# Stick-breaking attention: the value matmuls of two heads alternate on the two column halves of the array

## What is computed

```python
def block(args):                       # a block of 128 queries
    qi, bi = args
    qpos = bi * Q_BLOCK + jnp.arange(Q_BLOCK)
    mask = kpos[None, :] < qpos[:, None]
    z = jnp.einsum('bhqd,bhkd->bhqk', qi, k).astype(jnp.float32) * scale
    log_nb = jnp.where(mask, jax.nn.log_sigmoid(-z), 0.0)
    after = lax.cumsum(log_nb, axis=3, reverse=True) - log_nb
    w = jnp.where(mask, jnp.exp(jax.nn.log_sigmoid(z) + after), 0.0)
    return jnp.einsum('bhqk,bhkd->bhqd', w.astype(v.dtype), v)
```

## Time and profile before

| | |
|---|---|
| median of 3 runs | 3063.53 us (3063.17 to 3065.2) |
| span of the profiled execution | 3056.8 us |
| TensorE matmul busy | 2955.9 us, 97% |
| TensorE weight loads busy | 2375.5 us, 78% |
| VectorE busy | 1472.0 us, 48% |
| ScalarE busy | 1001.0 us, 33% |

### The profile page before, as it was taken

The page is one execution under the profiler, slowest core; times in us unless marked ns, Lnnn a source line. Parts: engine busy times, 40 slices in busy tenths (PEclk is TensorE's granted clock), DMA queues, the critical chain, the costliest instruction groups (busy, mean ns, idle before and its releaser), DMA issues. The chain is left out here.

```text
span 3056.8 us, 34380 instructions
## 1 busy us (share of the span) xinstructions
PE 2955.9 (97%) x13458; PEld 2375.5 (78%) x13458; DVE 1472.0 (48%) x1905; ACT 1001.0 (33%) x1128; POOL 32.7 (1%) x66
## 2 busy tenths in 40 slices
PE   7999999999999999999998999998999999899998
PEld 6888887478888888888776888887867567778886
DVE  6664346356743476433434444435444853443333
ACT  4222226332222322223444322224433343232222
POOL 0000000000000000000000000000000000000000
PEclk9999999899999999999999999999999999999999
DMA  4332222024333343222110222222321012222222
GB/s 161 137 131 97 106 103 82 0 96 139 136 104 110 110 144 132 93 105 85 56 42 28 96 96 96 96 102 106 131 92 64 28 55 97 83 83 96 96 102 77
DMA packets 44376, 289.99 MB, mean 95 GB/s; under 512 B 5136, under 2 KB 5520, under 8 KB 12928
## 3 DMA queue, kind: packets, MB, share of 16 engines
q1 hardware_dynamic: 35712, 259.01, 23.4%
q0 software_dynamic: 8000, 29.50, 2.9%
q10 hardware_dynamic: 576, 0.23, 0.0%
HBM read 286.62 MB, written 2.10 MB: 94 GB/s over the span
## 5 line engine op out<-in xcount | busy, mean ns | idle before, releaser
L802 DVE TENSOR_TENSOR sb_WL<-sb_RAW,sb_WH 128x2048 fp32r<-128x2048 f32 x243 | 556.8, 2291 | 891.3 <-ACT sb_WH L324 891.3
L1469 PE MATMUL PS<-sb_HH,sb_WH 128*128 128x512 f32 x2360 | 937.7, 397 | 33.8 <-DVE sb_WL L802 23.3
L1471 PE MATMUL PS<-sb_HH,sb_WL 128*128 128x512 f32 x2360 | 923.6, 391 | 0.0
L1470 PE MATMUL PS<-sb_HL,sb_WH 128*128 128x512 f32 x2360 | 923.4, 391 | 0.0
L324 ACT ACTIVATE sb_WH<-sb_RAW 128x2048 fp32r<-128x2048 f32 x243 | 464.8, 1913 | 785.1 <-PE PS L1471 783.2
L1469 PEld LDWEIGHTS PS<-sb_HH,sb_WH 128*128 128x128 f32 x2360 | 446.5, 189 | 139.6 <-issue 41.8
L1470 PEld LDWEIGHTS PS<-sb_HL,sb_WH 128*128 128x128 f32 x2360 | 446.4, 189 | 96.2 <-issue 5.0
L1471 PEld LDWEIGHTS PS<-sb_HH,sb_WL 128*128 128x128 f32 x2360 | 445.9, 189 | 94.6
L1469 PE MATMUL PS<-ff_GH,sb_WH 128*128 128x512 f32 x880 | 342.3, 389 | 0.0
L1470 PE MATMUL PS<-ff_GL,sb_WH 128*128 128x512 f32 x880 | 342.3, 389 | 0.0
L1471 PE MATMUL PS<-ff_GH,sb_WL 128*128 128x512 f32 x880 | 342.3, 389 | 0.0
(11 more groups left out here) (340 smaller groups left out, 2758.2 us busy)
## 6 DMA issues: line engine op xcount, KB each, us to landing
sb_RAW<-in_weights SPq DMA_DIRECT2D x243, 1024.0 KB, 4.8
ff_ADAW<-in_w_ada POOLq DMA_DIRECT2D x48, 512.0 KB, 4.0
sb_XT<-in_x SPq DMA_DIRECT2D x1, 2048.0 KB, 8.6
out_t<-sb_XT SPq DMA_DIRECT2D x4, 512.0 KB, 2.7
b_CT<-in_ctx POOLq DMA_DIRECT2D x1, 1024.0 KB, 5.0
hy_BD<-in_c_gates POOLq DMA_DIRECT2D x1, 512.0 KB, 3.4
hy_PT<-in_c_sel_fox POOLq DMA_DIRECT2D x1, 512.0 KB, 4.4
b_ROPE<-in_c_rope POOLq DMA_DIRECT2D x1, 512.0 KB, 6.3
```

What stands on the lines that cost most here:

```text
L802: dve.tensor_tensor(WL[slot][:, :], RAW[slot][:, :], f32(WH[slot][:, :]), ALU.subtract).then_inc(*T["w_lo"].up())
L1469: pe.matmul(out, wh, xh, start=start, stop=False)
L1470: pe.matmul(out, wh, xl, start=False, stop=False)
L1471: return pe.matmul(out, wl, xh, start=False, stop=stop)
```

## The change

The value matmuls are issued for two heads at once. `sb_values(q)` takes the heads 2q and 2q+1: for each key tile j it issues first the even head's matmul, then the odd head's, and one semaphore increment at the end. It is called in even passes h from 2 on, for q = h/2 - 1, and after the loop for the last pair. It stands where values(h-1) stood in those passes; in odd passes no value matmuls are left. `W` has three buffers in place of two, and the waits on `sb_o` count pairs: the Exp of head h waits for the pair of head h-3.

```diff
--- before.py
+++ after.py
@@ -134,7 +134,7 @@
                            ("I", [P, 4, S], F32), ("PT", [P, 2, TB, S], F32), ("BD", [P, 8, P], F32), ("B64", [P, P], F32),
                            ("MASK", [P, P], F32R), ("SEL", [P, 8, P], F32R), ("EYE", [P, P], F32R), ("ST", [P, 2, 2 * TB], F32)])
         sbm = layout("sbm", [("Q", [P, 8, S], F32), ("K", [P, 8, S], F32), ("V", [P, TB, D], F32), ("E", [P, 2, 1280], F32),
-                             ("SH", [P, 2, 1280], F32R), ("SL", [P, 2, 1280], F32R), ("W", [P, 2, 1280], F32), ("TRI", [P, P], F32R),
+                             ("SH", [P, 2, 1280], F32R), ("SL", [P, 2, 1280], F32R), ("W", [P, 3, 1280], F32), ("TRI", [P, P], F32R),
                              ("NONE", [P, P], F32R), ("MASK", [P, P], F32R), ("EYE", [P, P], F32R)])
         hyy = layout("hyy", [("YL0", [P, 4, S + 4], F32R), ("YH0", [P, 4, S], F32R), ("YH1", [P, 4, S], F32R), ("YL1", [P, 4, S], F32R)])
         HY_YH = [hyy["YH0"][:, m, :] for m in range(4)] + [hyy["YH1"][:, m, :] for m in range(4)]
@@ -591,13 +591,13 @@
                 act.wait_ge(T["sb_tri"].sem, h + 1)
                 if h == 0:
                     act.wait_ge(*T["sb_const"].now())
-                if h >= 2:
-                    act.wait_ge(T["sb_o"].sem, h - 1)
-                act.activation(sbm["W"][:, h % 2, :], zs(h)[:, 0:1280], ACT.Exp).then_inc(*T["sb_exp"].up())
+                if h >= 3:
+                    act.wait_ge(T["sb_o"].sem, (h - 3) // 2 + 1)
+                act.activation(sbm["W"][:, h % 3, :], zs(h)[:, 0:1280], ACT.Exp).then_inc(*T["sb_exp"].up())
 
             def sb_out(h):
                 if h % 2:
-                    act.wait_ge(T["sb_o"].sem, h + 1)
+                    act.wait_ge(T["sb_o"].sem, h // 2 + 1)
                     act.activation(sby["YH"][:, h // 2, :], PS[:, 6, :], ACT.Copy).then_inc(*T["y_hi"].up())
 
             split(U_SB + 1)
@@ -1719,13 +1719,19 @@
                                              start=False, stop=True, skip_group_check=True)
                 last.then_inc(*T["sb_tri"].up())
 
-            def sb_values(h):
-                pe.wait_ge(T["sb_exp"].sem, h + 1)
-                if h % 4 == 0:
-                    pe.wait_ge(T["evac"].sem, EV["sb"] + 3 * (h // 4) + 3)
-                if h >= 2 and h % 2 == 0:
-                    pe.wait_ge(T["y_ready"].sem, 8 + h // 2)
-                values(6, h, sbm["V"], lambda j: sbm["W"][:, h % 2, OFF[j]:OFF[j] + S - P * j], None).then_inc(*T["sb_o"].up())
+            def sb_values(q):
+
+                pe.wait_ge(T["sb_exp"].sem, 2 * q + 2)
+                if q % 2 == 0:
+                    pe.wait_ge(T["evac"].sem, EV["sb"] + 3 * (q // 2) + 3)
+                if q:
+                    pe.wait_ge(T["y_ready"].sem, 8 + q)
+                for j in range(TB):
+                    for e in range(2):
+                        h = 2 * q + e
+                        last = pe.matmul(PS[64 * e:64 * e + 64, 6, P * j:S], sbm["V"][:, j, HD * h:HD * h + HD],
+                                         sbm["W"][:, h % 3, OFF[j]:OFF[j] + S - P * j], start=j == 0, stop=True, skip_group_check=True)
+                last.then_inc(*T["sb_o"].up())
 
             sb_scores(0)
             for h in range(SBH):
@@ -1737,9 +1743,9 @@
                 sb_logs(h)
                 for k, s in halves[1:]:
                     half(k, s)
-                if h >= 1:
-                    sb_values(h - 1)
-            sb_values(SBH - 1)
+                if h >= 2 and h % 2 == 0:
+                    sb_values(h // 2 - 1)
+            sb_values(SBH // 2 - 1)
             pe.wait_ge(T["y_ready"].sem, 16)
             residual(RES["sb"], U_SBO, (8,), sby["YH"], sby["YL"], True)
             ffn(3)
```

## The result

The changed kernel is slower: median 3071.63 us (3066.85 to 3078.02, 6 runs) against 3063.35 us, a ratio of 1.0032 with a 95% interval of 1.0019 to 1.0045. A second set of 6 runs gave 1.0032 again (1.0014 to 1.0051). I had forecast 3057.2 us, range 3053.5 to 3064.0, with a chance of 0.11 for slower.

The account below looks back on a forecast made before the run. TensorE, busy 97% of the span, was taken to bound the kernel. Passes 1 to 11 gave -4.85 us and the last four heads -1.46, so 3063.5 - 6.3 = 3057.2 us, range 3053.5 to 3064.

Parts of the forecast that it names:

- One values block, two heads in one block: Values matmuls: one head's block takes 2.29 us; two heads on separate array halves stream together in 2.40 us.
- rivals B and D: Pair's values block: B, program order, 2.72 us, chance 0.13; D, no overlap, 4.44 us, chance 0.09.
- What it uncovers: Odd passes: scores wait 1.4 us for the Exp, starting 4.19 after logs, so each saves only 0.90 us.
- The clock: TensorE's clock at the new pauses: the sum counted no fall from them, so no cost.
- rival C: Six new 1.4 us pauses and one in pass 13 bring the clock down, 3.4 us per fall; chance 0.09.
- my -4.85: Passes 1 to 11: odd passes save 5.40 us, even passes 2 to 10 add 0.55.
- The last four heads: Passes 12 on and after the loop: +0.11, -2.72, +0.11, -0.06 and +1.1 for half clock on scores(15), together -1.46 us.
- Sum: Whole kernel: -4.85 - 1.46 = -6.3 us, taken from the median 3063.5, giving 3057.2 us.

Follow-up runs that it names:

- With the clock held: Changed kernel with 6 unread matmuls in each pause after logs(h), h odd up to 13: median 3060.11 us, ratio 0.9976 to the kernel before.
- the first profile: Beside +5.58, the changed kernel's first profile (median of its runs 3071.63 us); as the base worked from, the kernel before's, span 3056.8 us.
- the second: Beside +0.87 and 17.1, the changed kernel again, unaltered, ratio 1.0032; where named of the kernel before or by span, that kernel profiled again, 3065.0 us.
- the pauses alone: Kernel before with values(h-1) ahead of logs(h) in passes 1 to 11, nothing alternating: median 3092.38 us, ratio 1.0084.

## Why the prediction was wrong

**One values block, two heads in one block.** Right. 2.31 us, forecast 2.40, and rivals B and D (2.72, 4.44) are out. What the trace of before showed at one place holds in all eight blocks of the changed kernel: the six that scores follow take 2.30 or 2.31 us to the start of these, the seventh's records 2.38, and the eighth's 4.53 at half clock.

**What it uncovers.** Right in length: seven pauses of 1.33 us, forecast 1.4; 4.20 us from logs to scores, forecast 4.19. With the clock held, the first part is 5.06 us shorter, forecast 4.85.

**The clock.** This is the step that failed. The sum put the clock's answer to the new pauses at nothing, and I gave rival C 0.09 because a pause of 1.25 us at 2403.52 had left the clock at 1.00. That row has 128-row matmuls on both sides; the last one ahead of it is

```profile
2401.87 0.40 PE L1471 MATMUL PS<-sb_HH,sb_WL 128*128 128x512 f32 x1
```

Mine were to be followed by scores on 64 rows. The same 1.33 us before a projection half was followed by a fall in 0 of 5 cases, before scores in 4 and 3 of 6. The price per fall was about right: falls of 6.8, 6.8 and 3.4 us are worth 8.5 us, and 8.5 on top of my -4.85 is +3.7, measured +2.85. The chance was wrong, and with it the sum.

**The last four heads.** Forecast -1.46, measured +5.58 in the first profile and +0.87 in the second, against the second profile of the kernel before. Half clock lasted 31.3 and 17.1 us there, 13.7 in the kernel before. Against the first profile, from which I worked, the terms come out so:

| stretch | before, us | changed, us | difference | forecast |
|---|---|---|---|---|
| scores(13) to logs(13) | 13.27 | 14.86 | +1.59 | +0.11 |
| to scores(15) | 8.46 | 5.42 | -3.04 | -2.72 |
| to logs(15) | 13.27 | 17.89 | +4.62 | +1.21 |
| to the start of the last copy | 8.41 | 11.29 | +2.88 | -0.06 |

The work moved as forecast; what is missing is half clock: I had let it last as before, plus 1.1 us for scores(15). The change puts a pause before scores(13), scores(15) and the last values, but that these pauses cause the longer half clock is not shown. Filling those before scores(13) and scores(15) in the changed kernel leaves 17.6 us of half clock in the tail, as much as the second profile has without filling (17.1). It is 13.7 us where the waits for the low part before logs(13) and logs(15) are shortened, and 3.4 where pauses are filled as well. Each one's share stays open, and so does why the tail of one kernel differs from run to run.

**Sum.** The span was 3056.8 and the median 3063.53, and I took the difference for start and end of the run. It isn't: the second profile's span is 1.7 us under its run (3063.3, 3065.0). The first profile was simply of a shorter run, one without half clock at the first scores. So 3057.2 set a gain worked out from a short run against a median of longer ones. And it hid from me, in the very rows that I worked from, that the 1.9 us pause before scores(0) is usually followed by a fall, in nine of the ten profiles that have it: the best evidence for rival C.

## What to carry to other kernels

Where the change takes work from between a producer and its consumer, list what TensorE will run right behind the new pause: a pause of 1.3 us before full-array projections cost no more than its own length here; before the scores matmuls on 64 rows six of them cost 25.9 us with their falls, three times their length. At 2.2 us the pause before full-array log sums came with a fall too. Move independent full-array work into the gap first, then merge. And hold the profiled run against the others before using it as the base: a span several microseconds under the median may be the clock, not overhead (here 6.7 us, of which 1.7 were overhead).

## What was unexpected of the hardware

- A pause of about 1.3 us ahead of 64-row float32 matmuls was followed by 3.4 to 13.7 us at 1.2 GHz: 4 and 3 times in 6 in the two profiles of the changed kernel, 6 times in 6 with the pauses alone. Ahead of full-array projections it was so in 0 of 5, and a 1.7 us wait ahead of the output projection in 0 of 7 profiles.
- Matmuls on the two column halves run at full pace side by side: 16 float32 records in the time of 8 (2.31 us against 2.29), and with all of one head's ahead of the other's the second still starts early (3.86 us, not the 4.44 worked out for one after the other).
- Matmuls whose result nobody reads shortened the kernel: six in each of seven pauses, 10 to 12 us against the changed kernel by the medians (3060.11 against 3070.42 and 3071.63).
